# Value projection first and token-major, gates and branches token-major, in a decoder layer on one core

## The reference

```
h      = rms_norm(x, g_mix_pre)
proj   = h @ w_in             # q,k,v | z,xBC,dt | sc_b,sc_c,sc_h | 3 gates of 2048
y_attn = attention(q, k, v, rel_bias)        # 8 heads of 128, causal, relative bias
y_ssm  = mamba2(z, xBC, dt, ...)             # 4 groups, ends in a gated group rms norm
y_sc   = sc_b * causal_conv3(sc_c * sc_h)
merged = sig(g_a)*(y_attn@w_br_attn) + sig(g_m)*(y_ssm@w_br_ssm) + sig(g_c)*(y_sc@w_br_conv)
x += rms_norm(merged @ w_out, g_mix_post)
x += rms_norm(relu(rms_norm(x) @ w_up)**2 @ w_down)
x += rms_norm(sigmoid(rms_norm(x) @ w_ple_gate) * (p @ w_ple_proj))
```

## Time and profile before

| what | value |
|---|---|
| median of three runs | 1934.91 us (1933.51 to 1939.14) |
| the profiled execution | 1937.6 us |
| its span, first to last instruction | 1936.0 us |
| TensorE busy in the span | 1892.9 us, 98% |
| VectorE, ScalarE busy | 1205.8 us (62%), 947.1 us (49%) |
| memory read | 361.60 MB, 189 GB/s over the span |

### The profile page before, as it was taken

The page is one execution under the profiler, slowest core; times in us unless marked ns, Lnnn a source line. Parts: engine busy times, 40 slices in busy tenths (PEclk is TensorE's granted clock), DMA queues, the critical chain, the costliest instruction groups (busy, mean ns, idle before and its releaser), DMA issues.

```text
span 1936.0 us, 28941 instructions
## 1 busy us (share of the span) xinstructions
PE 1892.9 (98%) x10166; PEld 1620.1 (84%) x10166; DVE 1205.8 (62%) x1405; ACT 947.1 (49%) x1125; POOL 75.1 (4%) x113
## 2 busy tenths in 40 slices
PE   6999999999999999999999999999999999999997
PEld 5888888888888888888888888888888888888885
DVE  7445555666666888876565576556555554565674
ACT  5445555555444655565444464334434443444463
POOL 1010000000000011110000000100000000000010
PEclk9999999999999999999999999999999999999998
DMA  6565555665565555545556556655655555556553
GB/s 214 194 233 180 174 173 173 203 207 186 177 192 186 196 173 182 186 158 192 183 186 225 177 183 228 203 189 178 200 190 182 192 194 191 187 177 197 178 185 125
DMA packets 99798, 364.51 MB, mean 188 GB/s; under 512 B 11400, under 2 KB 11544, under 8 KB 99320
## 3 DMA queue, kind: packets, MB, share of 16 engines
q1 hardware_dynamic: 96624, 351.32, 55.3%
q0 software_dynamic: 2960, 12.36, 1.9%
q10 hardware_dynamic: 160, 0.12, 0.0%
HBM read 361.60 MB, written 3.70 MB: 189 GB/s over the span
## 4 chain that ended last, share of the span: by engine, by line
PE 93%; DVE 2%; ACT 2%; issue 1%; DMA 0%; POOL 0%; DVEq 0%; SPq 0%; ACTq 0%; POOLq 0%
PE ps L1374 43%; PE ps L1376 22%; PE ps L1392 9%; PE ps L1393 9%; PE ps L1394 9%; DVE w_lo L654 1%; ACT w_hi L308 1%; PE ps L1519 0%; DMA x_T<-x_in 0%; DVE xs L828 0%; POOL group_sq L1325 0%; POOL group_sq L1322 0%; DVE x_tok L1239 0%; PE ps L1521 0%; PE ps L1435 0%
## 5 line engine op out<-in xcount | busy, mean ns | idle before, releaser
L1374 PE MATMUL ps<-act,w_hi 128*128 128x512 f32 x3472 | 1228.7, 399 | 6.9 <-DVE act L684 5.8
L654 DVE TENSOR_TENSOR w_lo<-w_raw,w_hi 128x1024 fp32r<-128x1024 f32 x662 | 818.6, 1246 | 522.7 <-ACT w_hi L308 519.2
L308 ACT ACTIVATE w_hi<-w_raw 128x1024 fp32r<-128x1024 f32 x662 | 691.9, 1056 | 595.5 <-PE ps L1376 335.0
L1376 PE MATMUL ps<-act,w_lo 128*128 128x256 f32 x3472 | 972.2, 280 | 0.0
L1374 PEld LDWEIGHTS ps<-act,w_hi 128*128 128x128 f32 x3472 | 653.4, 188 | 166.1 <-DVE act L684 6.6
L1376 PEld LDWEIGHTS ps<-act,w_lo 128*128 128x128 f32 x3472 | 656.1, 189 | 0.2
L1392 PE MATMUL ps<-w_hi,act 128*128 128x512 f32 x768 | 299.4, 390 | 1.5 <-DVE act L1084 1.5
L1394 PE MATMUL ps<-w_hi,act 128*128 128x512 f32 x768 | 298.9, 389 | 0.0
L1393 PE MATMUL ps<-w_lo,act 128*128 128x512 f32 x768 | 298.8, 389 | 0.0
L1392 PEld LDWEIGHTS ps<-w_hi,act 128*128 128x128 f32 x768 | 144.1, 188 | 32.4 <-issue 1.7
L1394 PEld LDWEIGHTS ps<-w_hi,act 128*128 128x128 f32 x768 | 144.1, 188 | 30.1
(11 more groups left out here) (208 smaller groups left out, 826.8 us busy)
## 6 DMA issues: line engine op xcount, KB each, us to landing
w_raw<-w_stream SPq DMA_DIRECT2D x662, 512.0 KB, 3.4
a_rows<-decay_rows POOLq DMA_DIRECT2D x8, 512.0 KB, 7.3
x_T<-x_in SPq DMA_DIRECT2D x4, 512.0 KB, 6.2
x_tok<-x_tok_in POOLq DMA_DIRECT2D x4, 512.0 KB, 5.0
out<-x_tok SPq DMA_DIRECT2D x3, 512.0 KB, 2.8
bias<-bias_rows POOLq DMA_DIRECT2D x8, 128.0 KB, 3.1
gain_mix<-gains_in POOLq DMA_DIRECT2D x1, 1024.0 KB, 7.7
gain_mlp<-gains_in POOLq DMA_DIRECT2D x1, 1024.0 KB, 8.7
```

What stands on the lines that cost most here:

```text
L308: act.activation(whi[:, s, :], raw[:, s, :], ACT.Copy).then_inc(hi_ready, 1)
L654: dve.tensor_tensor(wlo[:, s, :], raw[:, s, :], whi[:, s, :], ALU.subtract)\
L1374: pe.matmul(out_, whi[:, s, at_:at_ + P], a.rearrange("p a t -> p (a t)"), start=first and i == 0, stop=False)
L1376: mm = pe.matmul(out_[:, T:2 * T], wlo[:, s, at_:at_ + P], a[:, 0, :], start=False, stop=last and i == len(kts) - 1)
```

## The change

- **v first.** A stage `v` of 16 token-major units (two blocks) comes before `qk` (32 units, feature-major as before). Its activations `act0` are x times the gain, not normalised; the two parts of 1/rms (`rs_col`, one number for each token, and `rs` for the rest) are worked out beside it, and `copy_v` multiplies the result by `rs_col`. v is then token-major already, and the transposes of v in attention are gone. TensorE starts with 24 float32 matmuls on a matrix of ones whose result nothing reads. SyncE loads quarters of x and units in turns.
- **Gates and branches token-major.** In `ga`, `gc`, `gm` and the last 8 units of `ssd` all units are token-major: gate blocks (8 units) go to bank pair 1, branch blocks (4 or 8 units) to pair 0. The sigmoid reads PSUM in one piece, VectorE multiplies from PSUM, and the adds of halves are gone. `merged` is token-major, so it is turned for `out` with 32 transposes (`turn_merged`).
- **Group sums.** GpSimd's adds are gone; `sum_group` is four float32 matmuls of 256 columns.

```diff
 STAGES = [
-    ("qkv", 48, 12),
+    ("v", 16, 0),
+    ("qk", 32, 8),
     ("att", 64, 16),
     ("dt", 2, 1),
-    ("ga", 48, 16),
-    ("gc", 48, 16),
+    ("ga", 48, 4),
+    ("gc", 48, 4),
...
             for i in range(4):
                 sp.dma_start(xT[:, 4 * i:4 * i + 4, :], x_in[:, 4 * i:4 * i + 4, :]).then_inc(x_loaded[i], 16)
-            for n in range(SLOTS):
-                sp.dma_start(raw[:, n, :], wstream[n]).then_inc(w_loaded[n], 16)
+                sp.dma_start(raw[:, i, :], wstream[i]).then_inc(w_loaded[i], 16)
...
# ScalarE, the start
+            split_x(0)
             split_hi(0, 0)
             split_hi(0, 1)
+            split_x(1)
             split_hi(0, 2)
+            for c in range(16):
+                step(0, c)
+                if c in (0, 2):
+                    split_x(2 + c // 2)
+                if c in (1, 2, 3, 4):
+                    square_x(c - 1)
...
# ScalarE, ga and gc
-                        if c in (3, 5, 9, 11):
-                            copy_right(it * 12, U + c, it * 4, B + (3, 5, 9, 11).index(c))
-                        if c in (4, 10):
-                            sigmoid_gate(c // 10, it * 4, B + 2 * (c // 10))
+                        if c == 8:
+                            sigmoid_gate(it * 12, U + 7, it, B)
...
# VectorE, the start
+            for c in range(16):
+                step(0, c)
+                if c in (0, 2):
+                    dve.wait_ge(x_loaded[2 + c // 2], 16)
+                    rest_x(2 + c // 2)
+                if c in (1, 2, 3, 4):
+                    add_squares(max(1, 2 * c - 2), 2 * c)
...
+                if c in (7, 9, 11, 13):
+                    norm_x(c // 2 - 3)
...
+            def gate_branch(ue, uc, ge, gates, n, first):
+                dve.wait_ge(unit_done, ue + (uc + 1))
+                dve.wait_ge(gate_ready, ge + gates)
                 if first:
+                    dve.tensor_tensor(merged[:, :, n], pair[0], gate, ALU.mult).then_inc(block_done, 1)
                     return
+                dve.tensor_tensor(rowbuf[:, :, :], pair[0], gate, ALU.mult).then_inc(branch_gated, 1)
+                dve.wait_ge(branch_gated, ge + (gates - 4))
+                dve.tensor_tensor(merged[:, :, n], merged[:, :, n], rowbuf[:, :, :], ALU.add)\
                    .then_inc(block_done, 1)
...
# TensorE
+            for i in range(24):
+                pe.matmul(bank[6][:, 0:P], ones[:, :], ones[:, :], start=True, stop=True)
+            for c in range(16):
+                rows_unit(0, c, act0, 2 * (c % 8), pair[c // 8], c % 8 == 0, c % 8 == 7, raw_x=c < 8)
+                if c == 5:
+                    pe.wait_ge(x_sq_added, 8)
...
-                        for k in range(2):
-                            mm = pe.transpose(bank[5][:, k * P:k * P + P], v_h[:, k * P:k * P + P], ident[:, :])
...
+            def gate_block(e, c, ge, gates):
+                if gates or not isinstance(ge, int):
+                    pe.wait_ge(gate_ready, ge + gates)
+                for j in range(8):
+                    rows_unit(e, c + j, act1, 2 * j, pair[1], j == 0, j == 7)
...
+                def gated_branch(it):
+                    gate_block(it * 12, U, it, 4 * i)
+                    pe.wait_ge(block_done, it + B)
+                    for j in range(4):
+                        rows_unit(it * 12, U + 8 + j, acts, 2 * j, pair[0], j == 0, j == 3)
...
             def sum_group(g):
-                pe.wait_ge(group_added, g * 2 + 2)
-                pe.matmul(bank[4][:, 0:T], ones[:, :], group_sq[:, 0, :], start=True, stop=True)\
+                pe.wait_ge(group_squared, g + 1)
+                for t in range(4):
+                    mm = pe.matmul(bank[4][:, 0:T], ones[:, :], group_sq[:, t, :], start=t == 0, stop=t == 3)
...
             U, B = UNIT0["gm"], BLOCK0["gm"]
+            for j in range(4):
+                pe.wait_ge(block_done, B + j)
+                for c in range(8):
+                    if j == 0 and c == 6:
+                        pe.wait_ge(y_ssm_lo, GROUPS)
+                    rows_unit(0, U + 16 * j + c, act2, 2 * c, pair[0], c == 0, c == 7)
+                    if j == 0 and c == 0:
+                        sum_group(GROUPS - 1)
+                if j < 3:
+                    pe.wait_ge(gate_ready, BRANCHES + j + 1)
+                    for c in range(8):
+                        rows_unit(0, U + 16 * j + 8 + c, act1, 2 * c, pair[1], c == 0, c == 7)
+                        if c == 3:
+                            turn_merged(j)
```

More of the change, by code:

```diff
@@ L120, in build @@
     w1 = region(16)
-    merged = place("merged", [P, DT, T], where=w1)
+    merged = place("merged", [P, 2, D], where=w1)
     y = place("y", [P, 2, D], where=w1)
@@ L268, in two, with m_bank @@
             return tensor[:, ds(2 * i, 2)]
[L270 removed]
+        BRANCHES = 8
+        UP_COPIES = BLOCK0["gm"] - BRANCHES
+        gate = ev.rearrange("p a b t -> p (a b t)").rearrange("p (k n) -> p k n", k=2)
+        def m_bank(j, odd):
+            return bank[4 + j % 2 * 2 + odd].rearrange("p (a t) -> p a t", a=2)
         NEXT = ("mlp", "ple")
@@ L434, in group_hi, with group @@
                 act.activation(act2[:, ds(g * 4, 4), 0, :], z[:, :, :], ACT.Copy).then_inc(y_ssm_hi, 1)
-            def group(g, first):
+            def group(g, first=False, last=False):
                 for c in range(16):
@@ L447, in group @@
                         group_hi(g - 1)
-                    if c % 4 == 3:
+                    if c % 4 == 3 and not (last and c > 8):
                         copy_right(g * 16, U + c, g * 4, B + c // 4)
@@ L719, in _, with rest_x, add_squares @@
-            with dve.Fori(1, 6) as it:
+            def rest_x(j):
+                for kt in range(4 * j, 4 * j + 4):
+                    dve.wait_ge(x_hi, kt + 1)
+                    dve.scalar_tensor_tensor(act0[:, kt, 1, :], xT[:, kt, :],
+                                             consts[:, G_MIX_PRE + kt:G_MIX_PRE + kt + 1], act0[:, kt, 0, :],
+                                             ALU.mult, ALU.subtract).then_inc(x_lo, 1)
+            def add_squares(first, end):
+                for b in range(first, end):
+                    dve.wait_ge(x_squared, b + 1)
+                    if b >= 2:
+                        dve.wait_ge(x_sq_added, b - 1)
+                    dve.tensor_tensor(x_sq[:, 0, :], x_sq[:, 0, :], x_sq[:, b, :], ALU.add).then_inc(x_sq_added, 1)
@@ new lines, in _ @@
+            for c in range(56):
+                step(0, U + c)
+                if c == 1:
+                    group_variance(GROUPS - 1)
+                if c == 2:
+                    group_norm(GROUPS - 1)
+                if c == 3:
+                    group_lo(GROUPS - 1)
+                if c % 16 == 12:
+                    merged_rest(c // 16)
+                if c % 16 == 7:
+                    j = c // 16
+                    gate_branch(0, U + c, 0, BRANCHES + j + 1, slice(512 * j, 512 * j + 512), first=False)
@@ L1378, in products, with rows_unit @@
                 return mm
-            def rows_unit(e, c, acts, kt, into, first, last, split=None):
+            def rows_unit(e, c, acts, kt, into, first, last, split=None, raw_x=False):
                 s = c % SLOTS
```

414 lines of the change are left out of this document (202 added, 212 removed).

## The result

| | before | after |
|---|---|---|
| median | 1934.29 us (4 runs, 1933.51 to 1939.14) | 1919.05 us (4 runs, 1918.68 to 1919.52) |
| the profiled execution, its span | 1937.6 us, 1936.0 us | 1919.52 us, 1917.7 us |

After over before is 0.9922, with a 95% interval of 0.9909 to 0.9935. The forecast was 1912.6 with a range of 1904 to 1921: the time lies in that range, but outside the 1909 to 1917 that the prediction gave its likeliest case alone. The gain of 15.2 us is two thirds of the 22.3 that the terms gave.

What follows compares the result with a forecast made beforehand. TensorE, busy 98% of the span, was taken to bound the kernel. The terms summed to -22.3 us, which taken off the median of 1934.9 gave 1912.6 us, range 1904 to 1921.

Steps and rivals of the forecast that it cites:

- Start: Kernel start: TensorE begins at 9.3, waits 3.7 us behind its sixth unit; unit 16 at 60.2 against 67.2, -7.0 us.
- the walk: Start, engine by engine: summed durations put VectorE's work before the sum of squares at 17.5 us, ending at 30.4.
- Attention: Attention: two transposes a head go, eight times 0.2 us, -1.6; GpSimd's wait before copying the next v is hidden.
- ga and gc: Gate and branch stages: 96 token-major units at 2.72 us, 261.1 against 271.3, -10.2; sigmoid and product hidden.
- Rivals 1 and 4: Token-major stages: either columns alone count, 1928 (5%), or TensorE waits for sigmoid and product on bank pairs, 1970 (4%).
- Group sums: Four group sums: 6.5 us of TensorE's waits for GpSimd go, extra float32 matmuls cost 5.3, -1.2 us.
- clock: The clock's fall behind the second wait for GpSimd should go with that wait, -1.7 us.
- last ssd units: Last 8 units of ssd, now token-major: 0.11 us less each, -0.9 us.
- No wait is next: Group sums: ScalarE's squares end at 704.25, before TensorE reaches the sum at 705.49, so no new wait follows.
- gm and merged: gm: 56 units from 2.77 to 2.72 us, -2.9; 32 transposes turning merged, +3.2, their wait and splits hidden.
- Rival 3: Start worth little: splits late from VectorE's normalising, 1 us at each of eight units or another clock fall; 1919, 15%.
- Rival 2: Start worth more: VectorE's adds take no TensorE time or the clock stays up; -12.5 instead of -7.0, 1907, 14%.

Runs made afterwards that it cites:

- sums_later: Changed kernel with the sums of squares on TensorE, and all that depends on them, behind the eighth unit instead of the sixth; 1912.64 us.
- gates_only: Kernel before with only the token-major gates and branches and the group sums on TensorE; start and attention as before; 1924.93 us.
- pool_adds: Changed kernel with the group sums' adds back on GpSimd and one float32 matmul; 1920.68 us.
- xdt_first: Changed kernel with VectorE's second decay segments moved behind xdt in each ssd group, their exponential one unit later on ScalarE; 1916.25 us.
- v_only: Kernel before with only the new stage v, act0, the start and no transposes of v; 1933.7 us, ratio 0.9981 to 1.0009.
- best: Changed kernel with sums two units later, xdt ahead of the second segments, and one unused transpose ahead of qk, up1, up2 and up3; 1904.76 us.
- before_pace: Kernel before with one unused transpose ahead of the second 8 units of qkv, of ga and of up1 to up3; 1930.53 us.
- before_again: Kernel before, unchanged, timed and profiled once more for its spread; 1933.48 us, ratio 0.9990 to 1.0021.
- pace: Changed kernel with 1, 2 and 8 unused transposes ahead of the second, third and fourth up projection; 1917.75 us.
- no_dummies: Changed kernel without the 24 float32 matmuls on ones ahead of the first unit; 1918.17 us.

## Why the prediction was right, and where it was off

Against the profiled execution the terms said -22.3 and -18.3 was measured in the span. By the terms:

- **Start, -7.0 forecast, -4.5 measured.** The mechanism came as written: one wait behind the sixth unit, for the last add of squares, and VectorE late by its own work. Two sizes were off. The walk's last add, 30.4, ended at 31.2; VectorE had stood idle for 1.2 ahead of the rest of unit 3 (16.96), until ScalarE had rounded it, and the walk had VectorE busy throughout. (The first weight matmul began at 10.09, not 9.3, since ScalarE's first high part waited for the gains, `consts`, to 6.10; but unit 1 came on time, so this costs the sum nothing. The dummies ended at 9.70, not 8.5, still ahead of it.) The larger miss is the clock: I priced its fall by the earlier trace rows at 3.4 us of half speed, 1.7 lost; it was 6.83 us, 3.4 lost. 0.8 and 1.7 are the 2.5 us. sums_later shows that wait and fall were 7.6 us, and could be had back.
- **Attention, -1.6 forecast, -1.2 measured.** 192.28 for 193.44. Right.
- **ga and gc, -10.2 forecast, -10.2 measured.** 261.14 for 271.30, and no wait for the sigmoid or the product. gates_only has the same 130.6 each, so it is this part of the change and not the others. The same stages took 2.83 us a unit in one form and 2.72 in the other. Rivals 1 and 4 fall. But 10.2 is the form together with the late pace: against feature-major units at the quick pace, 2.772, token-major ones win 0.052 a unit, 5.0 in 96, and the other 5.2 are there only because ga and gc ran late in this execution. A unit streams the same columns either way, with 16 matmuls in one form and 12 in the other (1538 and 1154 in the two windows). If the four matmuls are the whole 0.052, one costs 13 ns beyond its columns; this is an estimate from those two unit times. The Trainium skill, page "TensorE: Matmul & The Clock Gate", section "Back-to-back issue gap", gives columns / 2.4 GHz plus 2.5 ns for an isolated matmul, and says that in a stream of weight loads and matmuls both set the spacing. The isolated rule would make the two forms nearly equal; the trace disagrees.
- **Group sums -1.2, clock -1.7, last ssd units -0.9; -2.7 measured in ssd.** Three of the four sums lie in ssd, with 5.5 of the 6.5 us of waits and 4.0 of the 5.3 of matmuls, so -4.1 of the forecast lies there, and +0.3 in gm. The waits for GpSimd went, and the fall with them. What the prediction left out is that VectorE's segments stand ahead of `xdt`: TensorE, no longer held at the head of a group, came to `xdt` earlier and waited 2.7 there, 1.3 more than before. That is nearly all of the 1.4 that are missing. pool_adds and xdt_first show it from both sides. "No wait is next" held for the squares, and it was carried no further: the prediction had no term for the waits later in the group.
- **gm and merged, -2.9 + 3.2 forecast, with the fourth group sum +0.6; +0.2 measured.** gm's 56 units of 2.72 and the 32 transposes at 0.8 for eight came as written, with three of the four groups of transposes in gm and one in `out` (87.97 for 87.07).
- **mlp, ple: nothing, and nothing measured** (817.38 for 817.39).

The second half of the miss is the step from the profiled execution to the median. The prediction took 22.3 off 1934.9, though the terms were made against an execution of 1937.6, on the ground that the clock's fall may or may not be in the runs. 1915.3 would have been the consistent figure. The kernel before spreads over 10 us; that its quick executions already had something of what the change gives, and the profiled one hadn't, is my explanation of this, and isn't shown. The changed kernel's profiled execution stands only 0.5 over its median. So of the 6.4 us between forecast and result, 2.7 are this step and 4.2 the terms, less 0.5.

Rival 3 had the time, 1919, but not the mechanism: TensorE waited for no weight rest between units 8 and 16. It allowed for "another fall of the clock", and a longer one is what came. Rival 2 was wrong for this kernel and right for sums_later, by its own condition: 12.1 us when the adds are no wait.

**What stays open.** Why one of two equal stages takes one pace and the other the other isn't explained. The runs show that what stands ahead of it can change it, and that one program can take either (gm in the two profiles of the kernel before). That the 10 us of spread before are these paces is an inference: two profiled executions differ by it in gm (2.5 us), and the spread shrinks with the number of feature-major units whose pace can change (before 10 us, v_only 5.6, gates_only 3.0, after 0.8, best 0.2). But so does the number of runs, 22, 10, 7, 4 and 5, and xdt_first has 2.4 in 5; and no quick execution of the kernel before was profiled. The two profiled executions of the kernel before and the one of before_pace (1937.6, 1940.16, 1936.74) all lie in the upper part of their spread. Whether the profiler has a part in that stays open, though v_only's profiled execution, 1933.26, lies below its median.

## What to carry to other kernels

When a wait on the bounding engine goes, list every later wait in the same loop body with its slack, since the time saved is first offered to the next of them. A short wait in a busy stretch costs its length and can cost a stretch at the lower clock, here 1.7 or 3.4 us more for 4.2, so it pays to move the waiting instruction two units on, even where the amount of work stays the same. Take a sum off the execution from which its durations come, and look at the spread of the kernel before ahead of choosing another base.

## What the runs showed of the hardware

- Feature-major units (a 512-column and a 256-column matmul in turn) have two paces at a granted clock of 1.00, 0.3465 and 0.3535 us a pair. Either held over 32 units of an up projection; in attention and ssd, with other matmuls between, units of 2.77 and 2.83 stand in one stage. One transpose, 0.1 us, ahead of 32 units went with a stage 1.6 us shorter at up1 and up3 and not at up2, in three kernels; two did at up2, eight didn't at up3. Token-major units (512 columns throughout) with nothing beside them had one pace, 2.720 us, in every kernel.
- The granted clock fell to 0.50 behind waits of 1.8 to 2.4 us for 3.4 us, and not behind each of them (of three waits of 1.8 or 1.9 us, two in pool_adds, v_only and before_pace, one before and in before_again). Behind 4.2 us it was down for 6.83 us in four kernels (the changed one, v_only, pool_adds, pace), and for half of that in a fifth (xdt_first). Behind waits of 1.1 us for `xdt` it didn't fall.
- At a cold start the matmuls take twice their time while the windows read a granted clock of 1.00: in no_dummies the first unit takes 5.14 us, and the window from 10 to 15 shows 1.00. The trace's clock record there begins with the rise to 1.00, at 15.0 us, and the window takes the time ahead of it as 1.00.

```profile
10.00:15.00 5.00, 5.00 (x12) 3.98 (x13) 3.17 (x6) 3.62 (x6) 3.61 (x18) 1.00 1.03 410
```

The distances of the matmuls are the surer sign there.
